# First conditioning block of a decoder step in two chunks of four row tiles, with six projection tiles begun on the first chunk

## The chip, the cores and the metric

One NeuronCore of a Trainium2 chip runs the whole program. The metric is device time in microseconds (us), the median of several runs; lower is better.

## What is computed

One inference step of a two-layer decoder on 256 prompt tokens and 8 sample tokens, in fp32, with model width 1024. The part in which the change lies is the start of layer 0:

```python
cs = jax.nn.silu(c)
mod = (cs @ w_ada[i] + b_ada[i])[:, None, :]
sh_m, sc_m, g_m, sh_f, sc_f, g_f = jnp.split(mod, 6, axis=-1)
h = rmsnorm(x, norm_mix[i]) * (1 + sc_m) + sh_m
u = h @ w_in                                # 1024 x 2560
a_b, a_c, a_x, b_v, b_g = jnp.split(u, [D_A, 2*D_A, 3*D_A, 3*D_A + D_B], axis=-1)
ya = a_b * causal_depthwise_conv(a_c * a_x, buf_a, w_conv_a)          # 3 taps
yb = causal_depthwise_conv(b_v * sigmoid(b_g), buf_b, w_conv_b)       # 31 taps
yb = silu(layernorm(yb + b_conv_b)) 
x = x + g_m * (concatenate([ya, yb]) @ w_out)
```

Then come a dense SwiGLU, layer 1 with a pooling mixer and a top-2-of-8 expert SwiGLU (352 MB of the 462 MB of weights that are read), and a last norm.

## The kernel before

**Layout.** Activations lie transposed: the 1024 features are eight *row tiles* of 128 partitions, and the 264 columns are 256 prompt and 8 sample tokens. `xT` holds x, `hT` the modulated h. A weight is the stationary operand (128x128), and `hT[:, k, :]` is streamed, eight k per output tile.

**Weights.** The list `schedule()` (lines 71 to 91) sets the order of PE's work and, through `weight_stream` (123 to 146), the order in which SyncE (SP) issues the weight transfers. Each transfer (a *unit*, 1 MB as a rule) goes into one of the 14 slots of `ring`; unit n is issued once PE has begun unit n-13, and PE waits in `unit()` for the landing.

**The first conditioning block.** `ada(0, 0, k)` (line 1331) multiplies the transposed conditioning (`csT`, 32 columns wide) with 2048 columns of `w_ada`, that is shift and scale of the first norm. For each of eight k it issues four matmuls of 512 columns into four 32-row strips of bank 7, which the array works on side by side. Each fp32 matmul leaves two records in the trace. After k = 7, ScalarE (ACT) copies the bank into `ada_part` (`ada_copy`, 698), PE turns it with four transposes (`ada_turn`, matmuls of line 1350), VectorE (DVE) adds the bias (`add_ada`, 905), makes the gain (896) and scales eight row tiles (`scaled`, 915), ACT adds the shift to each (`shifts`, 678), and GpSimd (POOL) does the same for the 8 sample columns of all row tiles in three steps (`sample_mod`, 589 to 592). Only then the first matmul of w_in (`gemm`, matmuls of line 1368) can start.

**What lies between.** Between the eight `ada` units PE turns x (`x_tile`, eight of three transposes, line 1266), the parameters (`params`), and the convolution states (`states`), and sums squares with eight matmuls on `ones` (`squares_sum`, 1325; called `norm0`). The squares are made by ACT in one instruction over all of xT (659), when all eight tiles are there; ACT and DVE take turns in copying these tiles. ACT makes `rstd` from the sums (Ln at 671, Exp at 673).

**The projection.** `IN_ORDER = (4, 3, 1, 2, 0)`: five blocks of four output tiles, 32 matmuls each. Block 4 is the gate of mixer B (ACT's Sigmoid, 721), block 3 its value; DVE multiplies them (958) and then runs the 31 taps of mixer B on four tiles (995 and 998), 124 long instructions, beside PE's blocks 1, 2, 0 and two more `ada` blocks. The next thing that PE does after block 0 is `ln_sum` (1317), which needs the last tap. DVE's part of the samples of mixer B (946 to 951, from the states) stands ahead of the wait for block 4.

**Banks.** Eight PSUM banks are given out by `bank_uses()` (166); `claim` lets PE wait until the last user of the bank has emptied it.

## Time and profile before

| | us |
|---|---|
| runs of before | 1412.27, 1413.80, 1414.83 (median 1413.8) |
| the profiled execution: its own time | 1411.49 |
| its span in the trace | 1409.7 |
| PE busy | 1332.8 (95%) |
| DVE busy | 231.0 (16%) |
| ACT busy | 124.6 (9%) |

The profile is of one execution. Its span is cut into slices, and for each of them the page shows how busy each engine was; a timeline lists what ran when, and a row in brackets tells how long an engine sat idle before it and what released it. A stretch of PE that is busy throughout is bound by PE. The clock that the throttle granted to PE is listed too, but a duration of a matmul of known shape is the better witness of it.

### The profile page before, as it was taken

What the parts mean: (1) busy time and instruction counts of PE and PEld (TensorE: products, weight loads), DVE (VectorE), ACT (ScalarE), POOL (GpSimd) and SP (SyncE); (2) the same over time, 40 slices, a digit from 0 to 9 for tenths busy, and PEclk for the clock granted to TensorE, in tenths of its full rate; (3) what the DMA queues carried; (4) which work ended last, traced back from release to release, by engine and by line L of the source; (5) the groups of instructions that cost most, each with busy time, mean ns of one, the idle gap of its engine ahead of it and who ended that gap; (6) DMA issues with size and microseconds to landing.
All of it is one profiled execution on the core that took longest, in us unless ns stands there. A gap on an engine that the chain in (4) does not pass through costs nothing.

```text
span 1409.7 us, 29559 instructions
## 1 busy us (share of the span) xinstructions
PE 1332.8 (95%) x13185; PEld 766.9 (54%) x13186; DVE 231.0 (16%) x657; ACT 124.6 (9%) x256; POOL 19.9 (1%) x122
## 2 busy tenths in 40 slices
PE   7999999999998999998799999769999989999986
PEld 3777788778885435535335466224346344346344
DVE  0297200001007110100101000101101001001102
ACT  2101310001005100000000000000000000000002
POOL 1000000000002000000000000000000000000000
PEclk9999999999999999999999999979999999999998
DMA  9999575557428799899976676899999999999992
GB/s 335 405 406 370 206 236 201 190 180 252 150 89 360 306 384 397 322 419 421 406 253 234 225 249 216 360 423 419 417 422 420 416 423 419 417 421 417 392 421 114
DMA packets 87876, 462.18 MB, mean 328 GB/s; under 512 B 8747, under 2 KB 12119, under 8 KB 52663
## 3 DMA queue, kind: packets, MB, share of 16 engines
q1 hardware_dynamic: 86257, 458.59, 82.9%
q8 instruction: 109, 1.79, 0.5%
q10 hardware_dynamic: 1494, 1.67, 0.4%
q14 instruction: 16, 0.13, 0.0%
HBM read 458.94 MB, written 2.24 MB: 327 GB/s over the span
## 4 chain that ended last, share of the span: by engine, by line
PE 84%; DMA 11%; issue 2%; ACT 1%; DVE 1%; POOL 1%; DVEq 0%; ACTq 0%; SPq 0%; POOLq 0%
PE bank L1620 35%; PE bank L1368 24%; PE bank L1649 13%; DMA ring<-in_w_exp_down_dram 10%; PE bank L1543 4%; PE bank L1337 2%; PE bank L1665 2%; PE bank L1587 1%; DMA ring<-in_w_exp_gate_dram 1%; PE bank L1325 1%; PE bank L1266 1%; PE bank L1490 0%; ACT MIX L849 0%; PE bank L1504 0%; PE bank L1317 0%
## 5 line engine op out<-in xcount | busy, mean ns | idle before, releaser
L1620 PE MATMUL bank<-ring,HT 128*32 128x384 f32 (+1 forms) x5376 | 517.0, 543 | 19.1 <-issue 7.8
L1620 PEld LDWEIGHTS bank<-ring,HT 128*32 128x32 f32 x5376 | 183.5, 110 | 340.9 <-issue 312.5
L1649 PE MATMUL bank<-ring,hid_t 128*32 128x256 f32 x4128 | 249.5, 390 | 28.9 <-DMA ring<-in_w_exp_down_dram 28.9
L1368 PE MATMUL bank<-HT,ring 128*128 128x264 f32 x1024 | 232.9, 389 | 2.5 <-POOL HT L592 2.5
L1368 PEld LDWEIGHTS bank<-HT,ring 128*128 128x128 f32 x1024 | 194.5, 191 | 44.1 <-issue 11.1
L1649 PEld LDWEIGHTS bank<-ring,hid_t 128*32 128x32 f32 x4128 | 132.9, 112 | 135.1 <-DMA ring<-in_w_exp_down_dram 37.1
L1368 PE MATMUL bank<-BIG,ring 128*128 128x264 f32 x480 | 108.0, 386 | 0.0
L1368 PEld LDWEIGHTS bank<-BIG,ring 128*128 128x128 f32 x480 | 91.1, 190 | 15.5
L1188 DVE TENSOR_TENSOR MIX<-bank,MIX 128x512 f32<-128x512 f32 (+1 forms) x42 | 26.2, 624 | 413.0 <-PE bank L1620 411.4
L1543 PE MATMUL bank<-HT,ROWS 128*128 128x160 f32 (+2 forms) x432 | 61.7, 298 | 1.5 <-DVE keys L1132 1.5
L1543 PEld LDWEIGHTS bank<-HT,ROWS 128*128 128x128 f32 x432 | 56.8, 195 | 10.4 <-issue 10.3
L817 ACT ACTIVATE MIX<-bank 128x512 f32<-128x512 f32 (+1 forms) x42 | 22.9, 544 | 397.4 <-PE bank L1620 396.9
L920 DVE SCALAR_TENSOR_TENSOR xT<-bank,mod,xT 128x256 f32<-128x256 f32 x64 | 30.0, 476 | 134.5 <-PE bank L1665 129.7
L1337 PE MATMUL bank<-ring,csT 128*32 128x512 f32 x384 | 48.7, 638 | 1.9 <-ACT csT L645 1.7
L995 DVE SCALAR_TENSOR_TENSOR MIX<-MIX,vec 128x256 f32<-128x256 f32 x120 | 47.8, 476 | 0.0
L1192 DVE COPY hid_t<-bank 128x512 f32<-128x512 f32 (+1 forms) x36 | 21.4, 631 | 146.4 <-PE bank L1587 146.4
L824 ACT ACTIVATE MIX<-bank 128x512 f32<-128x512 f32 (+1 forms) x9 | 4.8, 549 | 422.6 <-PE bank L1649 422.6
L1649 PE MATMUL bank<-ring,MIX 128*32 128x256 f32 x576 | 39.9, 379 | 0.0
L1037 DVE TENSOR_TENSOR BIG<-bank,BIG 128x264 f32<-128x264 f32 x22 | 9.5, 432 | 161.8 <-PE bank L1368 161.8
L1649 PEld LDWEIGHTS bank<-ring,MIX 128*32 128x32 f32 x576 | 18.7, 110 | 12.4
L1587 PEld LDWEIGHTS bank<-ident,MIX 128*128 128x128 f32 x147 | 19.0, 206 | 11.2 <-issue 11.2
L1337 PEld LDWEIGHTS bank<-ring,csT 128*32 128x32 f32 x384 | 10.9, 113 | 25.7 <-issue 22.0
(203 smaller groups left out, 402.8 us busy)
## 6 DMA issues: line engine op xcount, KB each, us to landing
ring<-in_w_exp_gate_dram SPq DMA_DIRECT2D x64, 1024.0 KB, 19.2
ring<-in_w_exp_up_dram SPq DMA_DIRECT2D x64, 1024.0 KB, 16.9
ring<-in_w_exp_down_dram SPq DMA_DIRECT2D x64, 1024.0 KB, 21.2
ring<-in_w_ada_dram SPq DMA_DIRECT2D x48, 1024.0 KB, 12.6
ring<-in_w_exp_gate_dram SPq DMA_DIRECT2D x64, 768.0 KB, 11.9
ring<-in_w_exp_up_dram SPq DMA_DIRECT2D x64, 768.0 KB, 18.1
ring<-in_w_exp_down_dram SPq DMA_DIRECT2D x32, 1536.0 KB, 22.5
ring<-in_w_in_dram SPq DMA_DIRECT2D x10, 1024.0 KB, 25.5
```

What stands on the lines that cost most here:

```text
L817: a.activation(sil[:, g, 0:cols], bank[gate_banks[g]][:, 0:cols], ACT.Silu).then_inc(on("silu_ready"), step_of(g, groups))
L920: v.scalar_tensor_tensor(xT[:, d, 0:NP], src[:, 0:NP], g[:, d, 0:1], xT[:, d, 0:NP], ALU.mult, ALU.add)
L995: ins = v.scalar_tensor_tensor(yb[:, t, 0:NP], src, v_conv_b[:, t, k:k + 1], yb[:, t, 0:NP], ALU.mult, ALU.add)
L1188: v.tensor_tensor(sil[:, g, 0:cols], bank[up_banks[g]][:, 0:cols], sil[:, g, 0:cols], ALU.mult).then_inc(on("hid_ready"), step_of(g, groups))
L1192: v.tensor_copy(hidT[s][g], bank[turn_banks[s][g]][:, 0:cols]).then_inc(on("hidT_ready"), step_of(g, groups))
L1337: ins = t_.matmul(b[32 * j:32 * j + 32, :], csT[:, k, :], w[:, j, :], start=(k == 0), stop=(k == DT - 1), skip_group_check=True)
L1368: ins = t_.matmul(banks_of[label][:, 0:NT], w[:, k, f * P:(f + 1) * P], src(k0 + k), start=(k0 + k == 0), stop=(k0 + k == k_tiles - 1))
L1543: ins = t_.matmul(bank[b][:, i * width:(i + 1) * width], h_rows[:, t, d * P:(d + 1) * P], pick[:, t, 0:width], start=(i == 0 and t == 0), ...
L1587: ins = t_.transpose(b[:, i * P:(i + 1) * P], sil[:, g, i:cols:tiles], ident[:])
L1620: ins = t_.matmul(bank[banks[g]][j * GRP:(j + 1) * GRP, 0:cols], xg[:, k, g * GRP:(g + 1) * GRP], w[:, j, :], start=(k == 0), stop=(k == D ...
L1649: ins = t_.matmul(b[j * GRP:(j + 1) * GRP, (g % 2) * DQ:(g % 2 + 1) * DQ], hidT[s][g][:, c0:c0 + GRP], w[:, jj, j * DQ:(j + 1) * DQ], star ...
L1665: ins = t_.matmul(bank[PLACE_BANKS[h][j]][:, 0:NT], out_rows[j * GRP:(j + 1) * GRP, g, h * P:(h + 1) * P], place[j * GRP:(j + 1) * GRP, g, ...
```

## The change

The first conditioning block is cut by row tile of the norm instead of by k. Chunk c (0 or 1) holds shift and scale of row tiles 4c to 4c+3: four units (`mod`), each with four k and 512 columns, in matmuls of 128 columns (16 for each unit, where `ada` had four of 512). Each chunk has its own copy, two transposes (`modturn`), bias, gain and scaling. Six tiles of w_in (the four of block 4, and tiles 2 and 3 of block 3) are brought in four units of two k each (`first`), over 768 columns, and each unit's twelve matmuls are issued as soon as the row tiles of h are there: `first` 0 and 1 work on chunk 0, 2 and 3 on chunk 1. The sample columns of h are done by DVE between the prompt's scalings, no longer by POOL. The states are turned after `first` 3, into banks 6 and 7, and their transfers are issued behind the twelfth unit. Block 3 keeps tiles 0 and 1. DVE multiplies tiles 2 and 3 of block 3 before its part on the states and tiles 0 and 1 after it. `norm0` now comes ahead of `params`; both use bank 1.

```diff
-IN_ORDER = (4, 3, 1, 2, 0)
+IN_ORDER = (3, 1, 2, 0)
+HALF = 4
+FIRST = (("in3_2", 0), ("in3_3", 1), ("in4_0", 2), ("in4_1", 3), ("in4_2", 4), ("in4_3", 5))
+FIRST_AT = 3 * BLK + BLK // 2
+
+
+def in_tiles(blk):
+    return [f"in{blk}_{t}" for t in range(2 if blk == 3 else 4)]
+
...
-    steps = [("cond",), ("ada", 0, 0, 0), ("x", 0), ("x", 1), ("x", 2), ("x", 3), ("ada", 0, 0, 1), ("x", 4), ("x", 5),
...
+    steps = [("cond",), ("mod", 0, 0), ("x", 0), ("x", 1), ("x", 2), ("x", 3), ("x", 4), ("x", 5), ("x", 6), ("x", 7),
+             ("mod", 0, 1), ("norm0",), ("params",), ("mod", 0, 2), ("mod", 0, 3), ("modturn", 0),
+             ("first", 0), ("mod", 1, 0), ("mod", 1, 1), ("first", 1), ("mod", 1, 2), ("mod", 1, 3), ("modturn", 1),
+             ("first", 2), ("first", 3), ("states",)]
     for i, blk in enumerate(IN_ORDER):
         steps.append(("in", blk))
...
-        elif step[0] in ("in", "down"):
-            block({"in": w_in, "down": w_down}[step[0]][0], step[1] * BLK)
+        elif step[0] == "mod":
+            _, c, u = step
+            rows = w_ada[0][(u % 2) * 4 * P:(u % 2 + 1) * 4 * P, (u // 2) * D + c * BLK:(u // 2) * D + (c + 1) * BLK]
+            units.append((rows.rearrange("(k p) n -> p k n", p=P), 4, BLK))
+        elif step[0] == "first":
+            rows = w_in[0][step[1] * 2 * P:(step[1] + 1) * 2 * P, FIRST_AT:FIRST_AT + len(FIRST) * P]
+            units.append((rows.rearrange("(k p) n -> p k n", p=P), 2, len(FIRST) * P))
+        elif step[0] == "in":
+            block(w_in[0], step[1] * BLK, len(in_tiles(step[1])) * P)
+        elif step[0] == "down":
+            block(w_down[0], step[1] * BLK)
...
         elif step[0] == "states":
-            u += [("state_b0", 4), ("state_b1", 5), ("state_a", 0)]
+            u += [("state_b0", 6), ("state_b1", 7), ("state_a", 6)]
...
+        elif step[0] == "mod":
+            if step[2] == 0:
+                u.append((f"mod{step[1]}", 7))
+        elif step[0] == "modturn":
+            u.append((f"modturn{step[1]}", 6))
+        elif step == ("first", 0):
+            u += list(FIRST)
+            turn[0] = 2
         elif step[0] == "in":
-            tiles(f"in{step[1]}_{t}" for t in range(4))
+            tiles(in_tiles(step[1]))
         elif step[0] == "out" and step[2] == 0:
...
-            weights(2)
-            weights(3)
-            weights(4)
+            for n in range(2, 12):
+                weights(n)
             sp.dma_start(state_b_rows[0:120, :, :], state_b[0].rearrange("b k d -> (b k) d").rearrange("(s p) d -> p s d", p=120)).then_inc(on("states_loaded"), 16)
             sp.dma_start(state_a_rows[0:2 * NS, :], state_a[0].rearrange("b k d -> (b k) d")).then_inc(on("states_loaded"), 16)
-            for n in range(5, UNITS0):
+            for n in range(12, UNITS0):
                 weights(n)
...
-            for n in range(4):
+            pool.wait_ge(on("hs0_ready"), 2)
+            pool.sem_inc(on("hs_ready"), 1)
+            for n in range(1, 4):
...
-            ada_copy(0, 0)
-            shifts(0)
+            for c in range(2):
+                if c:
+                    b, n = plan["modturn0"]
+                    act.wait_ge(filled[b], n)
+                empty(f"mod{c}", a.activation(ada_part[:, 0:2 * P], wait_bank(f"mod{c}")[:, 0:2 * P], ACT.Copy))
+                shifts(0, c * HALF, (c + 1) * HALF)
+            for t in range(CT):
+                empty(f"in4_{t}", a.activation(gate_b[:, t, :], wait_bank(f"in4_{t}")[:, 0:NT], ACT.Sigmoid))
+                landed(f"in4_{t}")
+            act.sem_inc(on("gate_b_ready"), 1)
+            states()
             act.dma_start(new_a_sample[0, :, 0:1, :], state_a[0, :, 1:2, :]).then_inc(on("stored"), 16)
...
-            add_ada(0, 0)
-            make_gain(0, v_mix[:, 0])
-            scaled(0)
-
+            for c in range(2):
+                label, here = f"modturn{c}", slice(c * HALF, (c + 1) * HALF)
+                src = wait_bank(label)[:, 0:2 * P].rearrange("p (s j c) -> p s j c", s=2, j=HALF)[:, :, :, 0:NC]
+                parts = mod[:, 0, 0:2 * DT, :].rearrange("p (s t) c -> p s t c", s=2)[:, :, here, :]
+                bias = bada[:, 0, 0:2 * DT].rearrange("p (s t) -> p s t", s=2)[:, :, here]
+                empty(label, v.tensor_tensor(parts, src, bias.unsqueeze(3).to_broadcast([P, 2, HALF, NC]), ALU.add))
+                landed(label)
+                v.scalar_tensor_tensor(gain[:, 0, here, :], scale_of(0)[:, here, :], 1.0,
...
+                dve.wait_ge(on("gain0_ready"), c + 1)
+                hs = hT[:, here, NP:NT]
+                v.tensor_tensor(hs, xT[:, here, NP:NT], gain[:, 0, here, 1:NC], ALU.mult).then_inc(on("hs0_scaled"), 1)
+                for d in range(c * HALF, (c + 1) * HALF):
+                    v.scalar_tensor_tensor(hT[:, d, 0:NP], xT[:, d, 0:NP], gain[:, 0, d, 0:1], rstd[:, 0:NP],
+                                           ALU.mult, ALU.mult).then_inc(on("scaled"), 1)
+                    if d % HALF == 0:
+                        dve.wait_ge(on("hs0_scaled"), 2 * c + 1)
+                        v.tensor_tensor(hs, hs, rstd[:, NP:NT].unsqueeze(1).to_broadcast([P, HALF, NS]),
+                                        ALU.mult).then_inc(on("hs0_scaled"), 1)
+                    elif d % HALF == 1:
+                        dve.wait_ge(on("hs0_scaled"), 2 * c + 2)
+                        v.tensor_tensor(hs, hs, shift_of(0)[:, here, 1:NC], ALU.add).then_inc(on("hs0_ready"), 1)
+            dve.sem_inc(on("gain_ready"), 1)
...
+            dve.wait_ge(on("pads_ready"), 1)
+            dve.wait_ge(on("gate_b_ready"), 1)
+            glu(2)
+            glu(3)
             dve.wait_ge(on("state_b_ready"), 1)
...
+            glu(0)
+            glu(1)
...
+            def mod_unit(c, u):
+
+                label = f"mod{c}"
+                b = claim(label) if u == 0 else bank[plan[label][0]]
+                w = unit()
+                part, k0 = u // 2, (u % 2) * 4
+                for k in range(4):
+                    for j in range(HALF):
+                        ins = t_.matmul(b[32 * j:32 * j + 32, part * P:(part + 1) * P], csT[:, k0 + k, :],
+                                        w[:, k, j * P:(j + 1) * P], start=(u == 0 and k == 0),
+                                        stop=(u % 2 == 1 and k == 3), skip_group_check=True)
+                        if k == 0 and j == 0:
+                            frees(ins)
+                if u == 3:
+                    fill(label, ins)
+
+            def mod_turn(c):
+
+                acc, label = f"mod{c}", f"modturn{c}"
+                pe.wait_ge(emptied[plan[acc][0]], plan[acc][1])
+                b = claim(label)
+                for s in range(2):
+                    ins = t_.transpose(b[:, s * P:(s + 1) * P], ada_part[:, s * P:(s + 1) * P], ident[:])
+                fill(label, ins)
+
+            def first(i):
+
+                w = unit()
+                for k in range(2 * i, 2 * i + 2):
+                    pe.wait_ge(on("hs0_ready"), k // HALF + 1)
+                    pe.wait_ge(on("h_ready"), k + 1)
+                    for f, (label, _) in enumerate(FIRST):
+                        b = claim(label) if k == 0 else bank[plan[label][0]]
+                        ins = t_.matmul(b[:, 0:NT], w[:, k % 2, f * P:(f + 1) * P], hT[:, k, :],
+                                        start=(k == 0), stop=(k == DT - 1))
+                        if k % 2 == 0 and f == 0:
+                            frees(ins)
+                        if k == DT - 1:
+                            fill(label, ins)
...
                 elif kind == "in":
-                    gemm([f"in{step[1]}_{t}" for t in range(4)], h_tile, DT, h_ready(0) if step[1] == IN_ORDER[0] else None)
+                    gemm(in_tiles(step[1]), h_tile, DT)
```

TensorE, between the transposes of x and the first weights behind `norm0`, with the waits. Before (L1266 is a transpose, L1337 `ada`, L1325 `norm0`):

```order
L1266 MATMUL bank3<-ident,ROWS 128x8
L1337 MATMUL bank7<-ring,csT 32x512 [waits ring2_loaded]
L1337 MATMUL bank7<-ring,csT 32x512 x3
L1266 MATMUL bank1<-ident,BIG 128x96 [waits bank1_emptied,vec_loaded]
L1266 MATMUL bank1<-ident,BIG 128x52
L1266 MATMUL bank1<-ident,BIG 128x124
L1266 MATMUL bank1<-ident,BIG 128x12
L1337 MATMUL bank7<-ring,csT 32x512 [waits ring3_loaded]
L1337 MATMUL bank7<-ring,csT 32x512 x3
L1337 MATMUL bank7<-ring,csT 32x512 [waits ring4_loaded]
L1337 MATMUL bank7<-ring,csT 32x512 x3
L1325 MATMUL bank1<-ROWS,ones 128x264 [waits sq_ready,bank1_emptied]
```

After (L1324 is a transpose, L1419 `mod`, L1383 `norm0`):

```order
L1324 MATMUL bank3<-ident,ROWS 128x8
L1419 MATMUL bank7<-ring,csT 32x128 [waits ring1_loaded]
L1419 MATMUL bank7<-ring,csT 32x128 x15
L1383 MATMUL bank1<-ROWS,ones 128x264 [waits sq_ready,bank1_emptied]
L1383 MATMUL bank1<-ROWS,ones 128x264 [waits sq_ready] x7
L1324 MATMUL bank1<-ident,BIG 128x96 [waits bank1_emptied,vec_loaded]
L1324 MATMUL bank1<-ident,BIG 128x52
L1324 MATMUL bank1<-ident,BIG 128x124
L1324 MATMUL bank1<-ident,BIG 128x12
L1419 MATMUL bank7<-ring,csT 32x128 [waits ring2_loaded]
L1419 MATMUL bank7<-ring,csT 32x128 x15
```

One conditioning unit stands between the last transpose of x and `norm0`, where three units and the parameters stood; the parameters now wait for bank 1 to be emptied of the sums of `norm0`.

TensorE, from the end of `norm0` to the convolution's projection. Before (L1350 turns the conditioning, L1368 is w_in, 128x120 and 128x16 are the states):

```order
L1325 MATMUL bank<-ROWS,ones 128x264 x8
L1337 MATMUL bank<-ring,csT 32x512 x4
L1266 MATMUL bank<-ident,BIG 128x120 x8
L1266 MATMUL bank<-ident,BIG 128x16 x4
L1337 MATMUL bank<-ring,csT 32x512 x8
L1350 MATMUL bank<-ident,ROWS 128x128 x4
L1368 MATMUL bank<-HT,ring 128x264 x64
L1337 MATMUL bank<-ring,csT 32x512 x32
```

After (L1433 turns the conditioning, L1444 is `first`, L1466 the rest of w_in):

```order
L1419 MATMUL bank<-ring,csT 32x128 x32
L1433 MATMUL bank<-ident,ROWS 128x128 x2
L1444 MATMUL bank<-HT,ring 128x264 x12
L1419 MATMUL bank<-ring,csT 32x128 x32
L1444 MATMUL bank<-HT,ring 128x264 x12
L1419 MATMUL bank<-ring,csT 32x128 x32
L1433 MATMUL bank<-ident,ROWS 128x128 x2
L1444 MATMUL bank<-HT,ring 128x264 x24
L1324 MATMUL bank<-ident,BIG 128x120 x8
L1324 MATMUL bank<-ident,BIG 128x16 x4
L1466 MATMUL bank<-HT,ring 128x264 x16
L1395 MATMUL bank<-ring,csT 32x512 x32
```

The 64 projection matmuls of one row are now 12, 12, 24 and 16, with four conditioning units among them and a second turn (of two, where one of four stood) ahead of the 24.

DVE, from the bias to the scaled row tiles. Before:

```order
L905 TENSOR_TENSOR mod<-bank,vec 128x144 [waits bank6_filled,rstd_ready]
L896 SCALAR_TENSOR_TENSOR gain<-mod,vec 128x72 [waits bank6_emptied]
L915 SCALAR_TENSOR_TENSOR HT<-xT,gain,rstd 128x256 [waits gain_ready]
L915 SCALAR_TENSOR_TENSOR HT<-xT,gain,rstd 128x256 x7
L946 TENSOR_TENSOR BIG<-MIX,vec 128x32x30 [waits state_b_ready]
```

After, the first chunk (the second follows in the same form):

```order
L977 TENSOR_TENSOR mod<-bank,vec 128x2x36 [waits bank6_filled,rstd_ready]
L979 SCALAR_TENSOR_TENSOR gain<-mod,vec 128x36 [waits bank6_emptied]
L984 TENSOR_TENSOR HT<-xT,gain 128x4x8 [waits gain0_ready]
L986 SCALAR_TENSOR_TENSOR HT<-xT,gain,rstd 128x256
L990 TENSOR_TENSOR HT<-HT,rstd 128x4x8 [waits hs0_scaled]
L986 SCALAR_TENSOR_TENSOR HT<-xT,gain,rstd 128x256
L994 TENSOR_TENSOR HT<-HT,mod 128x4x8 [waits hs0_scaled]
L986 SCALAR_TENSOR_TENSOR HT<-xT,gain,rstd 128x256 x2
L977 TENSOR_TENSOR mod<-bank,vec 128x2x36 [waits bank6_filled]
```

The three steps on the samples have moved from POOL into DVE's row, and the second bias waits for bank 6, that is for PE's second turn.

## Rows read from the trace of the kernel before

**Rows 1.** Page: PE's busy tenths and DMA share in 40 slices of 35.2 us.

```profile
PE   7999999999998999998799999769999989999986
DMA  9999575557428799899976676899999999999992
```

**Rows 2.** Windows: length, PE, PEld, DVE, ACT, POOL busy (instructions), granted clock, DMA, GB/s.

```profile
10.00:20.00 10.00, 9.76 (x39) 3.94 (x39) 1.47 (x4) 1.37 (x4) 0.00 (x0) 1.00 1.04 376
20.00:30.00 10.00, 10.00 (x46) 4.62 (x46) 0.96 (x3) 3.64 (x3) 0.00 (x0) 1.00 1.04 321
```

**Rows 3.** Timeline, PE to 35 us: start, length, engine, line, instruction, records.

```profile
10.24 1.93 PE L1337 MATMUL bank<-ring,csT 128*32 128x512 f32 x8 [1.67 <-ACT csT L645]
12.11 3.35 PE L1266 MATMUL bank<-ident,ROWS 128*128 128x128 f32 x12
20.54 1.94 PE L1337 MATMUL bank<-ring,csT 128*32 128x512 f32 x8
22.40 1.30 PE L1266 MATMUL bank<-ident,BIG 96*128 96x96 f32 x4
23.64 3.06 PE L1337 MATMUL bank<-ring,csT 128*32 128x512 f32 x16
26.62 3.83 PE L1325 MATMUL bank<-ROWS,ones 128*128 128x264 f32 x16
31.38 1.39 PE L1266 MATMUL bank<-ident,BIG 120*128 120x120 f32 x12
34.00 1.06 PE L1337 MATMUL bank<-ring,csT 128*32 128x512 f32 x8 [0.24 <-DMA ring<-in_w_ada_dram]
```

**Rows 4.** Timeline, ACT ahead of and behind `norm0`, one small DVE step.

```profile
22.43 1.97 ACT L659 ACTIVATE ROWS<-xT 128x2112 f32<-128x2112 f32 x1
30.49 0.48 ACT L671 ACTIVATE rstd<-bank,eps 128x264 f32<-128x264 f32 x1 [6.09 <-PE bank L1325]
66.29 0.16 DVE L959 TENSOR_TENSOR MIX<-bank,BIG 128x8 f32<-128x8 f32 x1
```

**Rows 5.** Timeline, from the last conditioning unit to the first projection matmul.

```profile
35.16 0.60 ACT L703 ACTIVATE ROWS<-bank 128x512 f32<-128x512 f32 x1 [1.44 <-PE bank L1337]
35.81 0.66 PE L1350 MATMUL bank<-ident,ROWS 128*128 128x128 f32 x4 [0.74 <-ACT ROWS L703]
36.57 0.31 DVE L905 TENSOR_TENSOR mod<-bank,vec 128x144 f32<-128x144 f32 x1 [12.08 <-PE bank L1350]
37.18 3.43 DVE L915 SCALAR_TENSOR_TENSOR HT<-xT,gain,rstd 128x256 f32<-128x256 f32 x8
38.37 0.37 POOL L592 TENSOR_TENSOR HT<-HT,mod 128x64 f32<-128x64 f32 x1
```

**Rows 6.** Chain of waits, 0 to 70 us: start, length, what.

```profile
39.00 30.41 PE bank L1368 x128
```

**Rows 7.** Windows of 1 us: the granted clock is the third number from the end.

```profile
39.00:40.00 1.00, 1.00 (x4) 0.83 (x5) 1.00 (x4) 1.00 (x4) 0.00 (x0) 0.81 1.06 389
40.00:41.00 1.00, 1.00 (x4) 0.80 (x3) 1.00 (x3) 1.00 (x3) 0.00 (x0) 0.50 1.05 387
43.00:44.00 1.00, 1.00 (x6) 0.87 (x5) 0.97 (x4) 0.68 (x1) 0.00 (x0) 0.98 0.99 406
```

**Rows 8.** Timeline, later conditioning block, block 1 and the last taps.

```profile
69.33 7.08 PE L1337 MATMUL bank<-ring,csT 128*32 128x512 f32 x64
69.79 0.13 PEld L1337 LDWEIGHTS bank<-ring,csT 128*32 128x32 f32 x4 [0.30 <-issue]
76.34 14.51 PE L1368 MATMUL bank<-HT,ring 128*128 128x264 f32 x64
115.51 11.16 DVE L995 SCALAR_TENSOR_TENSOR MIX<-MIX,vec 128x256 f32<-128x256 f32 x28
127.24 1.95 PE L1317 MATMUL bank<-MIX,ones 128*128 128x264 f32 x8
```

**Rows 9.** Chain of waits in order of time, the experts' down projection.

```profile
540.01 10.36 PE bank L1649 x192
```

More of the change, by code:

```diff
@@ L673, in root_mean, with shifts @@
                 a.activation(rstd[:], rstd[:], ACT.Exp, scale=-0.5).then_inc(on("rstd_ready"), 1)
-            def shifts(n):
-                for d in range(DT):
+            def shifts(n, first=0, last=DT):
+                for d in range(first, last):
                     act.wait_ge(on("scaled"), n * DT + d + 1)
@@ L682, in _ @@
             root_mean(0)
-            for j in range(2):
-                src = wait_bank(f"state_b{j}")[:, 0:480].rearrange("p (t b k) -> p t b k", t=2, b=NS)
-                for t in range(2):
-                    ins = a.activation(st_b[:, 2 * j + t, :, 0:KB - 1], src[:, t], ACT.Copy)
-                empty(f"state_b{j}", ins)
-            for j in range(2):
-                landed(f"state_b{j}")
-            act.sem_inc(on("state_b_ready"), 1)
-            for t in range(CT):
-                src = wait_bank("state_a")[:, 0:64].rearrange("p (t b k) -> p t b k", t=CT, b=NS)
-                ins = a.activation(st_a[:, t, :, 0:KA - 1], src[:, t], ACT.Copy)
@@ L694, in _, with states @@
-            empty("state_a", ins)
-            landed("state_a")
-            act.sem_inc(on("state_a_ready"), 1)
+            def states():
+                for j in range(2):
+                    src = wait_bank(f"state_b{j}")[:, 0:480].rearrange("p (t b k) -> p t b k", t=2, b=NS)
+                    for t in range(2):
+                        ins = a.activation(st_b[:, 2 * j + t, :, 0:KB - 1], src[:, t], ACT.Copy)
+                    empty(f"state_b{j}", ins)
+                for j in range(2):
+                    landed(f"state_b{j}")
+                act.sem_inc(on("state_b_ready"), 1)
+                for t in range(CT):
+                    src = wait_bank("state_a")[:, 0:64].rearrange("p (t b k) -> p t b k", t=CT, b=NS)
+                    ins = a.activation(st_a[:, t, :, 0:KA - 1], src[:, t], ACT.Copy)
+                empty("state_a", ins)
+                landed("state_a")
+                act.sem_inc(on("state_a_ready"), 1)
@@ L718, in _ @@
                     continue
-                elif step[1] == 4:
-                    for t in range(CT):
-                        empty(f"in4_{t}", a.activation(gate_b[:, t, :], wait_bank(f"in4_{t}")[:, 0:NT], ACT.Sigmoid))
-                        landed(f"in4_{t}")
-                    act.sem_inc(on("gate_b_ready"), 1)
                 elif step[1] == 1:
@@ new lines, in _, with glu @@
+            dve.sem_inc(on("gain_ready"), 1)
+            def glu(t):
+                label = f"in3_{t}"
+                src = wait_bank(label)
+                v.tensor_tensor(up_b[:, t, KB - 1:], src[:, 0:NP], gate_b[:, t, 0:NP], ALU.mult)
+                empty(label, v.tensor_tensor(st_b[:, t, :, KB - 1], src[:, NP:NT], gate_b[:, t, NP:NT], ALU.mult))
+                landed(label)
+            dve.wait_ge(on("pads_ready"), 1)
+            dve.wait_ge(on("gate_b_ready"), 1)
+            glu(2)
@@ L1441, in _ @@
                     squares_sum(0, 0, DT)
+                elif kind == "mod":
+                    mod_unit(*step[1:])
+                elif kind == "modturn":
+                    mod_turn(step[1])
+                elif kind == "first":
+                    first(step[1])
                 elif kind == "in":
-                    gemm([f"in{step[1]}_{t}" for t in range(4)], h_tile, DT, h_ready(0) if step[1] == IN_ORDER[0] else None)
+                    gemm(in_tiles(step[1]), h_tile, DT)
                 elif kind == "ln_sum":
```

29 lines of the change are left out of this document (10 added, 19 removed).

## Prediction

> **What bounds the kernel now.** I began with the page's slices: PE is busy in tenths of 9 nearly everywhere, only the first slice has a 7, while the DMA share is a full 9 in the first four slices and then falls to 2 in the twelfth [rows 1]. So the start could be bound by either, and what comes later has slack in DMA at about 400 us: a shift of PE there passes on whole, since the ring is full and each transfer is issued by PE's progress. What the change is worth is read from the first 70 us.
>
> There the windows show PE busy for 9.76 of 10 us and then for all 10 us, with DMA at 376 and 321 GB/s [rows 2]. The timeline says how the two meet: PE goes without a hole from 12.11 us (x tiles, conditioning units, `params`, `norm0`, states) to the last conditioning unit, which waits for its transfer for 0.24 us only, at 34.00 [rows 3]. Transfers and PE finish the first conditioning block together. Then PE has 3.93 us with nothing but a turn in it (35.07 to 39.00): copy 0.60, turn 0.66, bias 0.31, gain, scaling, POOL's third step ending at 38.74 [rows 5]. From 39.00 the 64 matmuls of blocks 4 and 3 run in one piece, 30.41 us, to 69.41 [rows 6]. 32 of them take 14.51 us later [rows 8], 0.453 us each, so 64 should take 29.0; the other 1.4 us went to the clock: granted at 0.81 from 39, 0.50 from 40, back at 43 [rows 7]. That is the 1.2 GHz level, which PE fell to after the gap.
>
> So the change can pay only if PE has room ahead of the transfers. It moves no work off PE: all conditioning units, x tiles, `norm0` and the same 64 matmuls stand before the end of block 3 in both kernels. I count PE's time to that end, 69.4 us before.
>
> **The change part by part.**
>
> *Wait for the squares.* The second four x tiles start when the first four are done (12.11 + 3.3), as one unit of 1.94 no longer stands between them; everything behind x comes some 1.86 us earlier. Before, x was done at 20.5, where the third unit began [rows 3]. The squares started at 22.43 and took 1.97 [rows 4], so they end at 22.5 now. PE finishes x at 18.7 and one unit of 1.94 at 20.6, and then `norm0` waits until 22.6: **+2.0**. Before, `params` and two units covered this (`norm0` began at 26.62 [rows 3]).
>
> *Clock under `norm0`.* The conditioning unit took 1.93 at 10.24 and 1.94 at 20.54, but 1.06 at 34.00; the pair at 23.64 took 3.06, between 3.88 and 2.12 [rows 3]. So PE was at 1.2 GHz until some 2.1 us into that pair, though granted is shown as 1.00 there [rows 2]; I trust the durations. `norm0` then ran at 2.4 GHz (3.83 with its tail). In the new order it begins at 22.6 behind one unit and an idle stretch, so at the low level. The rise came 2.1 us after the start of steady matmuls in the one case, 4.0 in the other (39.0 to 43.0 [rows 7]); half of that is lost, 1.0 to 2.0, and 3.6 if all of `norm0` runs low: **+1.5**. A row says more: 3.35 us of transposes at 12.11, and as many again ahead of 20.54, left the unit behind them at 1.94 [rows 3]. The Trainium skill says so too ("TensorE: Matmul & The Clock Gate", Part 4: PE-mode transpose): transposes don't count as PE activity for the clock. By that rule, and the trace agrees, the eight x tiles in a row don't help. Were it otherwise, `norm0` would run at 2.4 GHz and the sum would be 3.5 in place of 5.0.
>
> *Bank 1.* `params` now claims the bank that Ln must empty first: 0.11 us to start and 0.48 to run [rows 4], **+0.65** on PE. `params` itself (1.24, low clock [rows 3]) may be as short as half: **-0.3** (0 to -0.6).
>
> *Conditioning units.* Before: three at 1.94, two in 3.06, three at 1.06, 12.05 together. After: 16 matmuls of 128 columns for each, the same product of columns. No row shows this shape. From below: at 2.4 GHz the arithmetic of the old unit was 7.08 us for eight [rows 8], 0.88 each, and at the low level twice that. From above: the nearest dense row with 32-column weights, 256 columns, has 192 records in 10.36 us [rows 9], 54 ns each; if that were a pace of issue, 32 records would be 1.73. Four weight loads take 0.13 [rows 8], and a unit now has eight rounds of four, 1.04. Weight loads overlap with matmuls, so I take 1.1, nearer to that row than to 54 ns, which fits 256 columns streamed and needs no issue limit. Two units at 1.94 and six at 1.1 are 10.5: **-1.5** (-3.4 to +2.2).
>
> *Two stalls for one.* The old gap of 3.93 had nothing of this block to fill it, and neither has the new one: behind the turn of chunk 0 PE has only `first` 0, behind that of chunk 1 only `first` 2. Each step is shorter: 0.1 to start, copy of 256 columns 0.4 (0.60 for 512), two turns 0.42 (four 0.66), 0.1, bias 0.25, gain 0.2, and then DVE's row up to the samples: three small steps of 0.16 [rows 4] and two scalings of 0.43 (3.43 for eight [rows 5]), 1.5 with the waits between, and 0.2 to PE. That is 3.2. The samples stand in DVE's row, so they push the third scaling back, but PE needs only the first ones. 2 x 3.2 - 3.93 = **+2.5** (2.8 to 3.9 each: +1.7 to +3.9).
>
> *Clock behind the stalls.* One fall before, 1.4 us. Now there are two gaps, each a little shorter than the one that let it fall: none, one or two falls. I take one: **0** (-1.4 to +1.4).
>
> *States.* Moved, not removed: 1.3 us of PE in either place. In the new place the third turn waits for bank 6, which ACT empties behind four Sigmoids: +0.4; the old wait of 0.24 for a transfer goes: **+0.2**. DVE's work on the samples of mixer B falls beside the 16 matmuls of the rest of block 3 (7.2 us) and is covered: two multiplications, then some 3.5 us. If the cover went, taps would start later, and DVE has only 0.6 us to lose: the last tap ends at 126.67, PE needs it at 127.24 [rows 8].
>
> *Transfers.* Up to the last unit of chunk 1 there are two more units of 0.79 MB and no states (0.5 MB): 1.05 MB, 2.7 us at some 387 GB/s [rows 7], landing near 36.7 instead of 34.0. PE asks for it near 50. Nothing waits for DMA.
>
> Sum: 2.0 + 1.5 + 0.65 - 0.3 - 1.5 + 2.5 + 0 + 0.2 = **+5.0 us** at the end of block 3, which comes at 74.4. Behind it the order on PE is the same, DVE's taps start from the same place, and the shift is carried to the end. The profiled execution took 1411.49, so 1416.5 there; it lies 2.3 below the median of the runs (1413.8), which gives **1418.8**. All low bounds together give 0, all high ones +14.
>
> **The rivals.**
>
> *It does what its form suggests.* Were transfers the only bound, chunk 1 would land at 36.7, one unit and one stall would bring `first` 2 to 41, and 24 matmuls (10.8), states and 16 matmuls (7.2) would end block 3 at 60.5: 9 us faster, **1405**. For it: DMA is at its full share there [rows 1]. Against: PE has no holes in which the 24 matmuls could go [rows 2, 3]. A part of it (2.8 or more) would need that low-clock time vanishes as well. 12 in 100, most of it for what I overlook.
>
> *Cheap chunks.* Units at 0.9, stalls at 2.8 and no fall of the clock: the sum falls to between 0 and +2.8, **1415**. For it: the gaps are shorter than 3.93. 20 in 100.
>
> *Issue of narrow matmuls decides.* If a record can't go faster than 54 ns [rows 9], units behind the first two take 1.73 and the sum is 5.0 + 3.7 = 8.7, **1422.5**; it decides from the point at which a unit at 2.4 GHz exceeds 1.1. With a second fall of the clock it reaches 1424. Slower than before either way. 13 in 100.
>
> **How the numbers follow.** The forecast, +2.8 to +8, has 55 in 100. About 0.2% (2.8 us) is what a measurement here can tell from no change. Slower by more: 55 + 13 = 0.68. Within it: 0.20. Faster: 0.12. The range leaves out most of the faster rival and the far end of the slower one: 1411.5 to 1424.5.
>
> **What would show it.** In the profile after: `norm0` waits for ACT for about 2 us and starts near 22.6; `params` waits some 0.6 us for ACT's Ln; two gaps of PE near 3.2 us, the first ending near 35, the second near 53; the unit of 16 matmuls at about 1.1 us at 2.4 GHz; block 3 ends at 74 in place of 69.4; no wait of PE for a transfer of `w_ada` or `w_in`. I am wrong if `first` 0 starts before 31, or if the wait ahead of `norm0` is missing, or if DVE's taps end later relative to PE.

## The result

| | before | after |
|---|---|---|
| median of seven runs | 1413.8 us | 1418.5 us |
| lowest and highest | 1412.27, 1415.96 | 1416.19, 1419.86 |
| profiled execution | 1411.49 | 1419.86 |
| its span | 1409.7 | 1418.1 |

The medians are 4.7 us apart, and the forecast was 1418.8. The ratio of the runs is 1.0029 with a 95% interval of 1.0017 to 1.0041, so slower by 4.1 us (2.4 to 5.8). The two profiled executions are further apart (8.4 us) than the medians, since before's lies below all of its seven timed runs and after's is the slowest of its seven. So the traces have to be compared stage by stage, and not by their ends.

Here is PE's timeline of the changed kernel (start, length, engine, line, instruction, records; in brackets the idle time before it and what ended it). It answers to [rows 3], [rows 5] and [rows 6]; line 1419 is a conditioning unit (32 records) or a pair of them (64), 1383 is `norm0`, 1433 the turn of a chunk, 1444 is `first`.

```profile
10.26 1.93 PE L1419 MATMUL bank<-ring,csT 128*32 128x128 f32 x32 [1.67 <-ACT csT L670]
12.12 6.63 PE L1324 MATMUL bank<-ident,ROWS 128*128 128x128 f32 x24
...
22.68 5.18 PE L1383 MATMUL bank<-ROWS,ones 128*128 128x264 f32 x16 [2.07 <-ACT ROWS L684]
...
28.53 0.88 PE L1324 MATMUL bank<-ident,BIG 96*128 96x96 f32 x4 [0.66 <-ACT rstd L696]
...
29.34 1.96 PE L1419 MATMUL bank<-ring,csT 128*32 128x128 f32 x64
...
31.80 0.44 PE L1433 MATMUL bank<-ident,ROWS 128*128 128x128 f32 x2 [0.51 <-ACT ROWS L737]
...
34.23 5.58 PE L1444 MATMUL bank<-HT,ring 128*128 128x264 f32 x24 [1.99 <-DVE HT L994]
...
39.73 1.95 PE L1419 MATMUL bank<-ring,csT 128*32 128x128 f32 x64
...
41.62 5.61 PE L1444 MATMUL bank<-HT,ring 128*128 128x264 f32 x24
...
47.16 1.95 PE L1419 MATMUL bank<-ring,csT 128*32 128x128 f32 x64
...
51.94 12.61 PE L1444 MATMUL bank<-HT,ring 128*128 128x264 f32 x48 [1.82 <-DVE HT L994]
```

The 1.67 us at the top stands in both kernels. Each other bracket is one of the predicted waits: 2.07 us for the squares, 0.66 for bank 1, and two gaps in which PE has a copy to wait for (0.51) and DVE's chain (1.99, then 1.82). No bracket names a transfer. The last row has 48 records in 12.61, where 24 took 5.58: a part ran at the low clock. The windows of 1 us show that (granted clock is the third number from the end):

```profile
52.00:53.00 1.00, 1.00 (x4) 0.82 (x5) 0.63 (x2) 1.00 (x3) 0.00 (x0) 0.89 1.06 434
53.00:54.00 1.00, 1.00 (x4) 0.78 (x3) 0.00 (x0) 0.98 (x2) 0.00 (x0) 0.50 0.98 410
```

Now where the shift is at each landmark. The chain of waits of the changed kernel, in order of time:

```profile
66.26 7.33 PE bank L1466 x32
...
134.41 7.12 PE bank L1466 x32
...
471.07 49.15 PE bank L1724 x480
...
692.10 83.79 PE bank L1724 x509
...
782.07 35.61 PE bank L1724 x440
...
1361.74 30.05 DMA ring<-in_w_exp_down_dram
```

Block 3 ends at 66.26 + 7.33 = 73.59, in place of 69.41: **+4.2**. The output projection starts at 134.41 in place of 129.19: +5.2. The first long row of the experts starts at 471.07 in place of 465.53: +5.5. The same pieces of before's chain are these:

```profile
129.19 7.12 PE bank L1368 x32
...
465.53 49.15 PE bank L1620 x480
...
685.38 82.28 PE bank L1620 x600
...
773.82 35.61 PE bank L1620 x440
...
1353.53 29.71 DMA ring<-in_w_exp_down_dram
```

From 465 to 774 before needed 308.3 us, after 311.0, for the same instructions; from there on the shift stays at 8.2. Of these 2.7 us, 1.5 lie in the long row (83.79 in place of 82.28), 0.8 in a wait for a down-projection transfer ahead of it (27.98 in place of 27.16) and 0.4 in a gap between them (7.80 in place of 7.43). The other traces tell whether the change is behind it. Late, order and keep, below, have the changed kernel's code in this stretch and needed 308.3, 308.4 and 308.7 us for it; bank, best, warm and warm2, with the same code there, needed 310.1 to 310.3. So it differs from trace to trace by 2 to 3 us under one and the same code, and what decides it is open. The shift of the medians, 4.7, is near the 5.2 to 5.5 at the landmarks ahead of the experts.

The one step without a forecast is that between block 3 and the output projection, another 1.0 us. It is a bank:

```profile
130.97 0.60 PE L1408 MATMUL bank<-ident,ROWS 128*128 128x128 f32 x4
131.13 1.45 DVE L1071 TENSOR_TENSOR BIG<-bank,BIG 128x264 f32<-128x264 f32 x4 [0.28 <-DVE MIX L1053]
...
132.39 1.80 PE L1375 MATMUL bank<-MIX,ones 128*128 128x264 f32 x7 [0.82 <-DVE BIG L1071]
```

The column sums (1375) go into bank 2. Before, block 0 lay in banks 4, 5, 0, 1, and they began at 127.24 [rows 8], 0.44 us behind the start of the turn:

```profile
126.80 0.60 PE L1350 MATMUL bank<-ident,ROWS 128*128 128x128 f32 x4
```

The new numbering puts block 0 into 0, 1, 2, 3, and PE has to wait until DVE has multiplied its third tile.

### The profile page after: what moved, and what is told of

Read it like the earlier page. It is cut to its first block, busy times and chain, and to the rows that moved or that the text cites. A ratio compares the mean times of both kernels' runs of the same rounds, so it can differ in the third digit from the quotient of the medians.

```text
span 1418.1 us, 29960 instructions
## 1 busy us (share of the span) xinstructions
PE 1335.8 (94%) x13377; PEld 774.4 (55%) x13378; DVE 232.0 (16%) x665; ACT 125.3 (9%) x257; POOL 18.5 (1%) x119
## 3 DMA queue, kind: packets, MB, share of 16 engines
q8 instruction: 111, 1.82, 0.5%
q10 hardware_dynamic: 1494, 1.67, 0.4%
## 4 chain that ended last, share of the span: by engine, by line
PE 81%; DMA 11%; DVE 5%; issue 2%; ACT 1%; POOL 0%; DVEq 0%; SPq 0%; ACTq 0%; POOLq 0%
PE bank L1724 35%; PE bank L1466 19%; PE bank L1753 13%; DMA ring<-in_w_exp_down_dram 10%; PE bank L1647 4%; DVE MIX L1053 3%; PE bank L1444 2%; PE bank L1769 2%; PE bank L1691 1%; PE bank L1383 1%; PE bank L1395 1%; DMA ring<-in_w_exp_gate_dram 1%; PE bank L1324 1%; PE bank L1419 1%; PE bank L1594 0%
## 5 line engine op out<-in xcount | busy, mean ns | idle before, releaser
L1466 PE MATMUL bank<-HT,ring 128*128 128x264 f32 x928 | 209.9, 387 | 0.0
L1466 PEld LDWEIGHTS bank<-HT,ring 128*128 128x128 f32 x928 | 175.2, 190 | 37.7 <-issue 8.4
L1466 PE MATMUL bank<-BIG,ring 128*128 128x264 f32 x480 | 108.0, 386 | 0.0
L1466 PEld LDWEIGHTS bank<-BIG,ring 128*128 128x128 f32 x480 | 91.1, 190 | 15.5
L1647 PEld LDWEIGHTS bank<-HT,ROWS 128*128 128x128 f32 x432 | 57.8, 197 | 10.8 <-issue 10.7
L1395 PE MATMUL bank<-ring,csT 128*32 128x512 f32 x320 | 36.6, 595 | 0.0
L1444 PE MATMUL bank<-HT,ring 128*128 128x264 f32 x96 | 23.8, 410 | 3.8 <-DVE HT L994 3.8
```

The costliest lines, as they stand in the source:

```text
L1395: ins = t_.matmul(b[32 * j:32 * j + 32, :], csT[:, k, :], w[:, j, :], start=(k == 0), stop=(k == DT - 1), skip_group_check=True)
L1444: ins = t_.matmul(b[:, 0:NT], w[:, k % 2, f * P:(f + 1) * P], hT[:, k, :], start=(k == 0), stop=(k == DT - 1))
L1466: ins = t_.matmul(banks_of[label][:, 0:NT], w[:, k, f * P:(f + 1) * P], src(k0 + k), start=(k0 + k == 0), stop=(k0 + k == k_tiles - 1))
L1647: ins = t_.matmul(bank[b][:, i * width:(i + 1) * width], h_rows[:, t, d * P:(d + 1) * P], pick[:, t, 0:width], start=(i == 0 and t == 0), ...
```

## Experiments

All are timed against the kernel before on the same chip; the changed kernel's ratio is 1.0029. Differences to the changed kernel are between medians of different batches (before's own median was 1413.58 in one and 1413.8 in the others).

**late: no projection on the first chunk alone.** The four units of chunk 1 and its turn come ahead of `first`.

```diff
-             ("first", 0), ("mod", 1, 0), ("mod", 1, 1), ("first", 1), ("mod", 1, 2), ("mod", 1, 3), ("modturn", 1),
-             ("first", 2), ("first", 3), ("states",)]
+             ("mod", 1, 0), ("mod", 1, 1), ("mod", 1, 2), ("mod", 1, 3), ("modturn", 1),
+             ("first", 0), ("first", 1), ("first", 2), ("first", 3), ("states",)]
```

> The changed kernel, but the four conditioning units of chunk 1 and their turn come ahead of all four `first` units, in PE's row and in the transfers; no projection work is begun on the first chunk alone. My theory (PE bounds the start, each stall behind a turn is paid, begun-early projections buy nothing): the first stall of 2.96 us is now covered by 3.9 us of units of chunk 1, only the second one (2.8) stays, so block 3 ends 2.9 us earlier than in the changed kernel (73.6), near 70.7, and the time is about 2.9 us lower, 1415.6. Rival (the transfers bound the start and the early projections hide behind them): PE would wait for the last units of chunk 1 and the 24 early matmuls (10.8 us) would come out into the open, block 3 ends near 80 and the time is slower than the changed kernel's, 1424 or more.

Measured: 1413.08, ratio 0.9997 (0.9988 to 1.0005), 5.4 us below the changed kernel and level with before. PE's timeline:

```profile
20.86 5.24 PE L1383 MATMUL bank<-ROWS,ones 128*128 128x264 f32 x16 [2.92 <-ACT ROWS L684]
...
30.40 3.70 PE L1419 MATMUL bank<-ring,csT 128*32 128x128 f32 x128
34.67 0.44 PE L1433 MATMUL bank<-ident,ROWS 128*128 128x128 f32 x2 [0.57 <-ACT ROWS L737]
34.94 21.54 PE L1444 MATMUL bank<-HT,ring 128*128 128x264 f32 x96
...
58.12 7.39 PE L1466 MATMUL bank<-HT,ring 128*128 128x264 f32 x32
```

The 96 records start right behind the second turn, with no wait at all, and run at full clock. I had expected the second stall to stay. That was a slip: `first` 0 and 1 need chunk 0 only, and while they run DVE and ACT make chunk 1. So both of DVE's chains are covered, and the fall of the clock behind them is gone too. From the end of `norm0` to the end of block 3 PE needs 39.3 us here and 45.7 in the changed kernel, 6.4 less. (The rest of the 8.1 us by which block 3 ends earlier lies ahead of the end of `norm0`: the x tiles took 4.81 in this execution in place of 6.63, and the unit behind them 1.08 in place of 1.94, so the clock was high.) This execution is the fastest of late's eleven, 1409.16, 3.9 us under their median, so the 8.1 us are not those of a typical one; the claim rests on the median, and on the waits that are gone. The rival, that transfers bound the start, is out: PE asked for the last unit of chunk 1 near 33 and had it, and the time is not above the changed kernel's. But the transfers do come into sight further on. At block 1, the 64 records of which start at 73.33, PE waits 0.82 us for `w_in`:

```profile
73.33 2.05 PE L1466 MATMUL bank<-HT,ring 128*128 128x264 f32 x8 [0.82 <-DMA ring<-in_w_in_dram]
```

**order: the wait for the squares covered.**

```diff
-             ("mod", 0, 1), ("norm0",), ("params",), ("mod", 0, 2), ("mod", 0, 3), ("modturn", 0),
+             ("mod", 0, 1), ("params",), ("mod", 0, 2), ("norm0",), ("mod", 0, 3), ("modturn", 0),
```

> The changed kernel, with `params` and the third conditioning unit ahead of `norm0` again. My theory: the 2.07 us in which PE waits for ACT's squares and the 0.66 us in which `params` waits for bank 1 go, block 3 ends 2.7 us earlier (70.9 in place of 73.6), and the time is 2.7 us lower, 1415.8. The clock rises with or under `norm0`, within 0.5 us of before. Rival (the clock decides: what is gained ahead of `norm0` is lost since it then runs at 1.2 GHz all through, 7.2 us): block 3 ends at 73 or later, time 1418.

Measured: 1417.05, ratio 1.0021 (1.001 to 1.0032), 1.5 us below the changed kernel. Both waits are gone, and `norm0` took 5.49 in place of 5.18:

```profile
20.55 1.30 PE L1324 MATMUL bank<-ident,BIG 96*128 96x96 f32 x4
21.79 1.94 PE L1419 MATMUL bank<-ring,csT 128*32 128x128 f32 x32
23.65 5.49 PE L1383 MATMUL bank<-ROWS,ones 128*128 128x264 f32 x16
...
33.08 7.27 PE L1444 MATMUL bank<-HT,ring 128*128 128x264 f32 x24 [1.99 <-DVE HT L994]
```

Block 3 ends at 72.4 by the chain of waits, 1.2 us earlier, not 2.7. The difference is where the rival has a point: `params` (1.30 for 0.88) and the unit (1.94 for 0.95) have moved ahead of `norm0`, to where PE still runs at 1.2 GHz. Of 2.7 us of wait, 1.4 was spent on that. And in this execution the clock fell behind the first gap (7.27 for 24 records) and not behind the second. The times come in two groups: ten of the twelve executions took 1416.3 to 1419.4, the other two 1410.9 and 1411.8. None of the two was profiled, so what sets them apart is open.

**keep: PE busy in the two gaps.**

```diff
+                for d in range(4):
+                    t_.matmul(bank[7][:, 0:NT], ones[:], sq[:, d, :], start=(d == 0), stop=(d == 3))
```

The two lines stand at the end of `mod_turn`, behind its `fill`.

> The changed kernel, with four matmuls of 264 columns behind each of the two turns of the chunks (8 more in all, 3.6 us of PE, into a bank that nobody reads, within the gaps of 2.0 and 1.8 us in which PE waits for DVE). My theory: the gap itself costs its length, and the clock that falls behind it costs 1.4 to 1.7 us more; with PE at work in the gap the clock stays at 2.4 GHz behind both gaps, the six tiles are done 1.4 us earlier than in the changed kernel, less 0.1 to 0.3 where the fillers end behind the gap. Time 1.2 us lower, 1417.3. Rival (the fall has to do with something else, or fillers come at full price): the granted clock still falls behind a gap, or block 3 ends later than 73.6.

Measured: 1418.55, ratio 1.0031 (1.0019 to 1.0043), no difference from the changed kernel that the runs can tell. The trace tells more:

```profile
22.66 6.79 PE L1383 MATMUL bank<-ROWS,ones 128*128 128x264 f32 x16 [2.06 <-ACT ROWS L684]
...
35.82 5.58 PE L1446 MATMUL bank<-HT,ring 128*128 128x264 f32 x24 [0.21 <-DVE HT L994]
...
53.53 10.92 PE L1446 MATMUL bank<-HT,ring 128*128 128x264 f32 x48
```

The last 48 records took 10.92 in place of 12.61, and no window behind `norm0` shows a granted clock under 1. So a fall costs 1.7 us. The three traces with bare gaps (the changed kernel, order and bank) show one fall each, behind the first gap or behind the second, and this one none. Since each of the two bare gaps also went by without a fall in one of those traces, one execution with fillers doesn't show that they avoid it. The fillers fit: from the end of `norm0` to `first` 0 it is 6.4 us in both kernels. But block 3 ended at 73.49, since `norm0` took 6.79 here and 5.18 there, the same instructions behind the same wait. So the clock ahead of the first gap varies between executions by as much as a fall costs, and one trace of each can't carry the claim that the fillers lower the median. They didn't, visibly.

**bank: block 0 back in banks 4, 5, 0, 1.**

```diff
- FIRST = (("in3_2", 0), ("in3_3", 1), ("in4_0", 2), ("in4_1", 3), ("in4_2", 4), ("in4_3", 5))
+ FIRST = (("in3_2", 4), ("in3_3", 5), ("in4_0", 0), ("in4_1", 1), ("in4_2", 2), ("in4_3", 3))
-            turn[0] = 2
+            turn[0] = 0
```

> The changed kernel, but `first` uses banks 4, 5, 0 to 3 and the count of tiles starts at 0, so that block 0 lies in banks 4, 5, 0, 1 again. My theory of the last 1.0 us of the shift: PE's column sums behind block 0 (`ln_sum`, bank 2) wait 0.82 us for DVE to empty the third tile of block 0. Expected: that wait is gone, `ln_sum` starts 0.4 us behind the turn in place of 1.4, the column sums start 1.0 us earlier at about 131.4, with the same start of block 3. Rival (DVE's last taps are late): the wait stays and is put down to the taps. The time should be 1.0 us lower, which the runs can hardly show; the trace decides.

Measured: 1417.9, ratio 1.003 (1.0018 to 1.0042), 0.6 us under the changed kernel's median and within its spread. The wait is gone:

```profile
129.18 0.60 PE L1408 MATMUL bank<-ident,ROWS 128*128 128x128 f32 x4
129.62 1.95 PE L1375 MATMUL bank<-MIX,ones 128*128 128x264 f32 x8
```

The column sums follow 0.44 us behind the turn, as before the change, and 1.42 in the changed kernel. Their start at 129.62 can't be set against the expected 131.4, since this execution had its x tiles at the high clock (4.80) and ended block 3 at 71.8. The distance from there is what counts: 57.8 us, as before (127.24 - 69.41), and 58.8 in the changed kernel. This execution is also the fastest of its six, as late's profiled one is of its eleven, and these are the two among the traces in the changed order of x tiles (the changed kernel, late, order, keep, bank and best) that had them at the high clock.

**carry: does a delay at the start reach the end?** The kernel before, with 16 more matmuls between blocks 4 and 3:

```diff
+                    if step[1] == 3:
+                        for k in range(2 * DT):
+                            t_.matmul(bank[7][:, 0:NT], ones[:], hT[:, k % DT, :], start=(k == 0), stop=(k == 2 * DT - 1))
```

> The kernel before, with 16 more matmuls of 264 columns on PE between blocks 4 and 3, into a bank that nobody reads. It measures whether a delay at the start reaches the end. They cost 7.2 us at block 3's end. My theory (DMA idles behind a full ring near 400 us, so everything behind shifts): +7.2 us, 1421.0. Rival (the experts' phase, in which DMA is at its full share for hundreds of us, swallows a part): +2 to +4 us, 1416 to 1418.

Measured: 1420.41, ratio 1.0049 (1.0036 to 1.0062), +6.8 us for 7.2 of work. In the chain of waits the pieces of 465.53, 773.82 and 1353.53 start at

```profile
474.37 49.15 PE bank L1623 x480
...
782.60 35.61 PE bank L1623 x440
...
1362.27 29.92 DMA ring<-in_w_exp_down_dram
```

that is 8.8, 8.8 and 8.7 later. (7.12 are the matmuls; the other 1.6 came from the clock at the start of this execution.) A delay at the start goes through 900 us of experts undiminished, though DMA is at its full share in most of them [rows 1].

**best: the repairs together.** `norm0` behind the third unit; the chunks' accumulators in banks 7 and 6; block 0 in the banks of the run bank; and the projections placed where they cover DVE's chains:

```diff
+             ("mod", 0, 1), ("params",), ("mod", 0, 2), ("norm0",), ("mod", 0, 3), ("mod", 1, 0), ("modturn", 0),
+             ("mod", 1, 1), ("mod", 1, 2), ("first", 0), ("first", 1), ("mod", 1, 3), ("first", 2), ("modturn", 1),
+             ("first", 3), ("first", 4), ("first", 5), ("first", 6), ("first", 7), ("states",)]
```

Here `first` is one k, and its transfers are still of two.

> All repairs together: `params` and the third unit ahead of `norm0`; the accumulators of the two chunks in banks 7 and 6, so that chunk 1 can begin before chunk 0 is copied; the turn of chunk 0 followed by two units of chunk 1, then `first` on row tiles 0 and 1, the last unit of chunk 1, row tile 2, the turn of chunk 1, row tiles 3 to 7; and the last projection block in banks 4, 5, 0, 1, so that the column sums behind it find bank 2 free. My theory: no stall over 0.5 us and no fall of the clock, block 3 ends near 64.4 (before 69.4, changed 73.6), time 1413.8 - 5.0 = 1408.8. Rival (transfers bound it as soon as PE no longer does): PE waits for the last unit of chunk 1, block 3 ends at 67 to 69, time 1411.5 to 1413.5.

Measured: 1410.73, ratio 0.9977 (0.9969 to 0.9986), 2.9 us below before on the same chip (1413.58), and 7.8 below the changed kernel. PE waits for nobody between 10.25 and the states; block 3 ends at 65.8 and not at 64.4, and `norm0` took 5.86 us, most of it at the low clock, where 3.83 were enough before [rows 3]. In the trace the end of block 3 and the column sums are each 3.6 us ahead of before's; the medians are 2.9 apart, and not the 5.0 that were expected.

```profile
23.64 5.86 PE L1385 MATMUL bank<-ROWS,ones 128*128 128x264 f32 x16
...
43.26 13.52 PE L1448 MATMUL bank<-HT,ring 128*128 128x264 f32 x60
```

**warm: the clock raised while PE has nothing to do.** Best, with 17 matmuls on `ones` ahead of the first real work, the second unit again between the x tiles, and `norm0` behind the fourth unit.

> The repaired kernel (label best) plus 17 matmuls of 128 columns on a constant while PE waits for the first data (13 before the conditioning is turned, 4 behind it), and the second conditioning unit again between the two groups of x tiles. My theory: PE reaches 2.4 GHz before 8 us, x tiles take 4.8 us in place of 6.6 for all eight, units 0.95 each, and block 3 ends 4 to 6 us earlier than in best (65.8), near 60 to 62. But then the transfers bound: the first weights of block 1 land near 73, PE asks for them at 68, and the wait of some 4 us gives the gain back: time within 1 us of best's. Rival (the transfers have room): no wait there, time 4 us or more below best's.

Measured: 1411.19, ratio 0.9982 (0.9974 to 0.9991). The time is as expected, 0.5 us from best. The x tiles took 2.16 for each half (3.35 before [rows 3]). But then PE got ahead of the transfers, waited, and the clock fell while it did, which I had not expected. So block 3 ended at 63.9, 1.9 us ahead of best and not 4 to 6, and this lead went at block 1 in two waits, 0.33 and 1.65 us, not 4:

```profile
14.13 2.16 PE L1326 MATMUL bank<-ident,ROWS 128*128 128x128 f32 x12
...
20.32 1.93 PE L1429 MATMUL bank<-ring,csT 128*32 128x128 f32 x32 [1.60 <-DMA ring<-in_w_ada_dram]
22.19 5.82 PE L1393 MATMUL bank<-ROWS,ones 128*128 128x264 f32 x16
...
73.04 2.27 PE L1478 MATMUL bank<-HT,ring 128*128 128x264 f32 x9 [1.65 <-DMA ring<-in_w_in_dram]
```

Here, then, is the point at which transfers bound the start: the first weights of block 1 land at 73.0 to 73.3, in this kernel as in late.

**warm2: those transfers asked for later.** Warm, with block 1 ahead of the second conditioning block:

```diff
-        if i in (0, 2):
-            late = ada_steps(0, 1 + i // 2)
-            steps += late[:DT]
-        elif i in (1, 3):
+        if i == 1:
+            late = ada_steps(0, 1)
+            steps += late[:DT]
+        elif i == 2:
+            steps.append(late[DT])
+            late = ada_steps(0, 2)
+            steps += late[:DT]
+        elif i == 3:
             steps.append(late[DT])
```

and in DVE's row `add_ada(0, 1)` after tap row 21 in place of 14.

> The kernel of label warm, with block 1 ahead of the second conditioning block, its turn behind block 2, and DVE's use of it after tap row 21 in place of 14. So 8 MB of transfers are asked for 14 us later. My theory: the wait for the weights of block 1 is gone, and the start is bound by PE again: column sums behind block 0 at 118 to 119.5 (best: 123.8), time 4 to 5 us below best's, 1406. Rival (transfers bind at the next place, the second or third conditioning block): PE waits for w_ada there, and 1 to 2 us are gained only.

Measured: 1406.61, ratio 0.9952 (0.994 to 0.9964), 7.2 us below before and 11.9 below the changed kernel, the fastest of all. The column sums start at 120.64 (best 123.64, before 127.24), a little later than expected, since PE still waits 1.8 us for transfers up to `first`:

```profile
PE bank L1460 <- DMA ring<-in_w_in_dram: 0.9, 1, 0.9
...
PE bank L1433 <- DMA ring<-in_w_ada_dram: 0.9, 2, 0.6
```

(From the list of who waited for whom: total, times, longest.) No wait for the weights of block 1 is left. Against warm (column sums at 123.94) this trace gains 3.3 us: 2.2 behind the end of block 3, where the two waits of 2.0 together are gone, and 1.1 ahead of it, where PE has the same program in both and clock and waits fell out otherwise (`norm0` took 3.83 in place of 5.82). The medians are 4.6 apart; the last 1.3 us of that can't be put down to a wait.

## Why the prediction was right, and where it was not

The sum was +5.0 at the end of block 3, and the trace has +4.2 there and +5.2 behind the column sums. The main step held: PE had no room ahead of the transfers, so work begun early displaces other work and brings nothing by itself, while the new waits come on top. Late showed it by taking the early work away and gaining 5.4 us. In the table each row of PE counts up to the start of the next one, so that, before rounding, the terms but the last add up to the 4.2 at the end of block 3:

| term | forecast | measured |
|---|---|---|
| wait for the squares | +2.0 | +2.07 |
| `norm0` at the low clock | +1.5 | +1.4 (5.19 for 3.76) |
| bank 1 | +0.65 | +0.66 |
| `params` | -0.3 | -0.4 (0.81 for 1.24) |
| conditioning units | -1.5 | -2.1 (9.58 for 11.71) |
| two stalls for one | +2.5 | +1.8 |
| clock behind the stalls | 0 | 0 (one fall in both, 1.7 each) |
| 64 matmuls in four rows | none | +0.5 (30.88 for 30.41) |
| states, old wait | +0.2 | +0.3 |
| bank 2, behind block 3 | none | +1.0 |

*Units.* Mis-sized: a pair of narrow units at 2.4 GHz takes 1.95 us, 0.97 each and not 1.1; the two at the low level took 1.93 and 1.94, as forecast. The unit lies near the 0.88 of arithmetic. The rival that narrow matmuls would be bound at 54 ns is out: a record takes 30 ns.

*Stalls.* The gaps were 2.94 and 2.83 us, not 3.2. I had counted DVE's row up to the samples at 1.5 us, its small steps at 0.16 each in sequence; it took 1.2 (32.84 to 34.02), since two of the three steps add 0.10 each, as the next scaling starts 0.1 us into them:

```profile
33.35 0.18 DVE L990 TENSOR_TENSOR HT<-HT,rstd 128x32 f32<-128x32 f32 x1
33.45 0.48 DVE L986 SCALAR_TENSOR_TENSOR HT<-xT,gain,rstd 128x256 f32<-128x256 f32 x1
```

*The fall.* The prediction put before's fall at 1.4 us, from 14.51 for 32 matmuls; that row's length includes an end that overlaps the next row. The chain of waits has 128 records of the same shape at 166.69 us in 28.68, so the fall cost 30.41 - 28.68 = 1.7, as in the changed kernel (12.61 for 10.92 in keep). What the prediction put at nothing is the cutting of the 64 matmuls into four rows, +0.5.

*Bank 2.* The step that failed is "behind it the order on PE is the same": the order is, the banks are not. I had followed the banks of the first block and not those of the tiles behind it. The missing +1.0 and +0.5 and the two terms that were too dear (1.3 together) cancelled, so the total was better than its parts, and that is luck.

*The clock* came out as taken, but by luck in part. It differs between executions of one program here: eight x tiles took 6.6 us in some and 4.8 in others, `norm0` 5.2 to 6.8, and a gap costs a fall of 1.7 or none. The prediction reasoned that if the x tiles did help the clock, `norm0` would run at 2.4 GHz and the sum be 3.5. In late and bank the clock was high behind the x tiles, and `norm0` took 5.24 all the same: PE reached the squares sooner, waited 2.92 us for them instead of 2.07, and the granted clock was at 0.50 when they came. In bank:

```profile
12.10 4.80 PE L1324 MATMUL bank<-ident,ROWS 128*128 128x128 f32 x24
16.83 1.08 PE L1419 MATMUL bank<-ring,csT 128*32 128x128 f32 x32
...
21.00:22.00 1.00, 1.00 (x3) 0.79 (x4) 0.00 (x0) 0.00 (x0) 0.00 (x0) 0.50 1.05 389
```

*A reading.* The prediction says that only the first of PE's slices has a 7; the twentieth and the twenty-sixth have one too, the twenty-seventh and the last a 6 [rows 1]. Nothing in the sum rests on it.

*Carried to the end*: right, and shown by carry. *No wait for a transfer*: right in the changed kernel. The faster rival, in which transfers bound the start, is not the state of either kernel, but it isn't far: with block 3 ending 8 us earlier, as in late's trace, `w_in` of block 1 comes 0.8 us late.

What stays open is why the profiled execution of the changed kernel lost another 2.7 us among the experts. Carry, with the same expert code as before, lost nothing there (308.2 us from 474.37 to 782.60), so it isn't a consequence of a delay as such; late, order and keep lost next to nothing with the changed kernel's expert code, so it isn't one of the change either. Open too is what decides the clock at the start, which moves whole executions by some us.

## What to carry to other kernels

Before beginning work early to hide it behind transfers, count whether the engine has holes while they run; where it is busy throughout, the reordering is only worth what it does to the waits. When a block is cut in two, its chain of small steps on other engines is paid twice, unless work that doesn't depend on it is placed right behind each turn: nearly the same pieces in another order gave 1418.5, 1413.1 and 1410.7 us. And when tiles are renumbered, follow the banks to the next fixed user, beyond the code that is touched.
